# Two-map attention with three score banks in turn, one bank for transpositions, negated scaled keys and one reciprocal per step

## The reference

```
def diff_attention(q, k, v, qn_g, kn_g, lam_vec, subln_g, lambda_init):
    q = partial_rope(rmsnorm(q, qn_g)) * (A_DIM ** -0.5)      # [B, T, 4 heads, 2 maps, 64]
    k = partial_rope(rmsnorm(k, kn_g))
    v = ...                                                   # [B, 4 heads, T, 128]
    lam = exp(sum(lv[0] * lv[1])) - exp(sum(lv[2] * lv[3])) + lambda_init
    for each block of 128 queries:
        s = einsum('bhcqd,bhckd->bhcqk', q_block, k)          # c: the two maps
        p = softmax(where(causal, s, NEG_BIG), axis=-1)
        a = p[:, :, 0] - lam * p[:, :, 1]
        o = einsum('bhqk,bhkv->bhqv', a, v)
    return rmsnorm(o, subln_g) * (1.0 - lambda_init)
```

## Time and profile before

| what | us |
|---|---|
| median of 3 runs (lowest to highest) | 3673.33 (3672.34 to 3683.07) |
| the profiled execution | 3681.57 |
| its span on the core | 3679.8 |
| mean granted TensorE clock | 0.963 of 2.4 GHz |
| first reduction of the stage to the end of its last copy out, layer 0 | 67.16 |
| the same, layer 1 | 65.92 |

### The profile page before, as it was taken

The page is one execution under the profiler, slowest core; times in us unless marked ns, Lnnn a source line. Parts: engine busy times, 40 slices in busy tenths (PEclk is TensorE's granted clock), DMA queues, the critical chain, the costliest instruction groups (busy, mean ns, idle before and its releaser), DMA issues.

```text
span 3679.8 us, 41482 instructions
## 1 busy us (share of the span) xinstructions
PE 3533.7 (96%) x16488; PEld 2783.2 (76%) x16488; DVE 1470.8 (40%) x2606; ACT 1008.7 (27%) x1246; POOL 1500.2 (41%) x505
## 2 busy tenths in 40 slices
PE   8999999799999999999999999988999999789999
PEld 7878777578887888765788876845888869448887
DVE  4454267844243423235311146765201267643010
ACT  2222222622223212204222233342212333422121
POOL 3444452035454545510355554402546445015453
PEclk9999998999999999999999999978999999779999
DMA  6434221024352434211223222201222212002222
GB/s 245 179 140 190 97 81 68 1 82 194 120 195 97 183 131 153 86 56 50 80 84 105 85 92 79 71 1 46 92 93 101 91 69 81 12 35 90 93 95 76
DMA packets 53867, 360.66 MB, mean 98 GB/s; under 512 B 5968, under 2 KB 6352, under 8 KB 16592
## 3 DMA queue, kind: packets, MB, share of 16 engines
q1 hardware_dynamic: 53712, 358.53, 26.6%
HBM read 356.41 MB, written 2.10 MB: 97 GB/s over the span
## 4 chain that ended last, share of the span: by engine, by line
PE 90%; DVE 6%; ACT 1%; issue 1%; DMA 1%; POOL 1%; SPq 0%; DVEq 0%; ACTq 0%; POOLq 0%
PE LP L500 79%; PE XB L500 9%; DVE S L2116 1%; PE XB L711 1%; DMA big<-w_ada 1%; PE LP L827 1%; POOL w_lo L1618 1%; ACT E L1172 1%; DVE tmp L2238 0%; DVE st L2236 0%; DVE gain L1951 0%; ACT sq L1172 0%; DVE wk L2136 0%; DVE stat L2128 0%; DVE ada_in L2605 0%
## 5 line engine op out<-in xcount | busy, mean ns | idle before, releaser
L1618 POOL TENSOR_TENSOR w_lo<-ring,w_hi 128x2048 fp32r<-128x2048 f32 (+1 forms) x263 | 1125.8, 4281 | 724.5 <-ACT w_hi L1172 724.1
L500 PE MATMUL LP<-u_hi,w_hi 128*128 128x512 f32 x2480 | 987.3, 398 | 17.7 <-ACT u_hi L1172 10.6
L500 PE MATMUL LP<-u_hi,w_lo 128*128 128x512 f32 x2480 | 975.0, 393 | 0.0
L500 PE MATMUL LP<-u_lo,w_hi 128*128 128x512 f32 x2480 | 947.7, 392 | 0.0
L500 PE MATMUL LP<-big_r,w_hi 128*128 128x512 f32 x2432 | 750.0, 389 | 1.2 <-POOL w_lo L1618 1.2
L1172 ACT ACTIVATE w_hi<-ring 128x2048 fp32r<-128x2048 f32 (+1 forms) x263 | 468.6, 1782 | 827.8 <-PE LP L500 734.2
L500 PE MATMUL LP<-big_r,w_lo 128*128 128x512 f32 x1472 | 576.4, 392 | 0.0
L500 PEld LDWEIGHTS LP<-u_hi,w_hi 128*128 128x128 f32 x2480 | 471.8, 190 | 133.0 <-issue 35.8
L500 PEld LDWEIGHTS LP<-u_hi,w_lo 128*128 128x128 f32 x2480 | 471.5, 190 | 101.1
L500 PEld LDWEIGHTS LP<-u_lo,w_hi 128*128 128x128 f32 x2480 | 470.1, 190 | 96.1 <-issue 0.5
L500 PEld LDWEIGHTS LP<-big_r,w_hi 128*128 128x128 f32 x2432 | 455.9, 188 | 95.7 <-issue 1.2
(11 more groups left out here) (306 smaller groups left out, 3622.2 us busy)
## 6 DMA issues: line engine op xcount, KB each, us to landing
ada_in<-w_ada SPq DMA_DIRECT2D x66, 1024.0 KB, 4.9
ring<-w_in SPq DMA_DIRECT2D x22, 1024.0 KB, 4.7
ring<-w_gu00a SPq DMA_DIRECT2D x11, 1024.0 KB, 7.2
ring<-w_gu00b SPq DMA_DIRECT2D x11, 1024.0 KB, 6.7
ring<-w_gu01a SPq DMA_DIRECT2D x11, 1024.0 KB, 6.8
ring<-w_gu01b SPq DMA_DIRECT2D x11, 1024.0 KB, 6.7
ring<-w_gu10a SPq DMA_DIRECT2D x11, 1024.0 KB, 6.8
ring<-w_gu10b SPq DMA_DIRECT2D x11, 1024.0 KB, 7.0
```

Source lines behind the costliest of these rows:

```text
L500: return pe.matmul(o, lhsT=lhsT, rhs=rhs, start=start, stop=stop)
L1618: gp.tensor_tensor(w_lo[:, slab % RING, 0:width], ring[:, slab % RING, 0:width], w_high(q, width).bitcast(F32), ALU.subtract).then_inc(s(" ...
```

## The change

The two-map attention gets functions of its own (`diff_attention`) on TensorE, ScalarE and VectorE, with their own semaphores; `attention` keeps the one-map case. What differs for the two maps:

- The scores go through three PSUM banks in turn (`XB[k % 3]`), and TensorE waits for the reduction of three maps before; all transpositions go to `XB[3]`, so that each waits for ScalarE's copy of the one before.
- The keys are multiplied by their gains and by -0.125 (L2490 has a second factor), and the causal mask is negated once; the reduction takes the minimum of the negated scaled scores, and that minimum serves as the bias of the exponential, whose scale is -1. The small instruction L2119 is gone, and with it the `link` behind the reduction.
- The two sums are inverted by one instruction on two columns; minus lambda is a second factor of the instruction that scales map 1.

```diff
-                            if k >= 2:
-                                pe.wait_ge(s("smax_done"), k - 1)
-                            score(hh, m, qb, XB[k % 2]).then_inc(s("scores_done"), 1)
+                            k = 2 * n + m
+                            if k >= 3:
+                                pe.wait_ge(s("diff_max"), u0 + k - 2)
+                            score(hh, m, qb, XB[k % 3]).then_inc(s("diff_scores"), 1)
...
-                        if k >= 2:
-                            pe.wait_ge(s("pt_done"), k - 1)
-                        pe.wait_ge(s("probs_done"), k + 1)
-                        src = wk[:, 4 + k % 2, :] if maps == 2 else E[:, k % 4, :]
+                        if i:
+                            pe.wait_ge(s("pt_done"), p0 + i)
+                        pe.wait_ge(s("probs_done"), p0 + i + 1)
                         for b in range(qb + 1):
-                            last = pe.transpose(XB[2 + k % 2][:, blk(b)], src[:, blk(b)], cc("ident"))
+                            last = pe.transpose(XB[3][:, blk(b)], wk[:, 4 + i % 2, blk(b)], cc("ident"))
...
+                        if n >= 2:
+                            act.wait_ge(s("probs_done"), p0 + n - 1)
+                        for m in range(2):
+                            k = 2 * n + m
+                            act.wait_ge(s("diff_max"), u0 + k + 1)
+                            f(E[:, k % 4, 0:W], S[:, m, 0:W], ACT.Exp, scale=-1.0, bias=stat[:, k % 4, 0:1],
+                              accum_out=stat[:, k % 4, 1:2]).then_inc(s("diff_exp"), 1)
...
+                        f(ET[:, i % 2, 0:W], XB[3][:, 0:W], ACT.Copy).then_inc(s("pt_done"), 1)
...
+                link(ts(cc("causal"), cc("causal"), -1.0, None, ALU.mult))
...
-                            link(dve.tensor_tensor_reduce(
-                                out=S[:, k % 2, 0:W], in0=XB[k % 2][:, 0:W], in1=mask(qb, W), scale=1.0,
-                                scalar=LOWEST, op0=ALU.add, op1=ALU.max, accum_out=stat[:, k % 4, 2:3]))
-                            ts(stat[:, k % 4, 0:1], stat[:, k % 4, 2:3], -scale, None, ALU.mult)\
-                                .then_inc(s("smax_done"), 1)
+                            dve.tensor_tensor_reduce(
+                                out=S[:, m, 0:W], in0=XB[k % 3][:, 0:W], in1=cc("causal", T - W, W), scale=1.0,
+                                scalar=-LOWEST, op0=ALU.add, op1=ALU.min, accum_out=stat[:, k % 4, 0:1])\
+                                .then_inc(s("diff_max"), 1)
...
-                            link(dve.reciprocal(stat[:, q % 4, 3:4], stat[:, q % 4, 1:2]))
-                            link(ts(stat[:, q % 4, 3:4], stat[:, q % 4, 3:4], lam, None, ALU.mult))
-                            link(ts(wk[:, 3, 0:W], E[:, 2 * k % 4, 0:W], stat[:, q0 % 4, 3:4], None, ALU.mult))
+                        link(dve.reciprocal(stat[:, e:e + 2, 3:4], stat[:, e:e + 2, 1:2]))
+                        link(ts(wk[:, 3, 0:W], E[:, e + 1, 0:W], stat[:, e + 1, 3:4], lam, ALU.mult, ALU.mult))
...
-                        ts(big[:, c:c + 2, :], LP[p][:, :, :], sp_("qn" if k < 3 else "kn", l), None, ALU.mult)\
+                        gains, sign = (sp_("qn", l), 1.0) if k < 3 else (sp_("kn", l), -0.125)
+                        ts(big[:, c:c + 2, :], LP[p][:, :, :], gains, sign, ALU.mult, ALU.mult)\
```

More of the change, by code:

```diff
@@ L682, in rotate, with diff_attention, attention @@
                 pl.rope += len(chunks)
-            def attention(heads, score, val, hd, maps=1, beside=None):
+            def diff_attention(l, score, val, beside):
+                n_units = DIFF_H * NB
+                u0, p0, h0 = 2 * l * n_units, pl.prob, pl.head
+                for n in range(n_units + 3):
+                    if n < n_units:
+                        hh, qb = divmod(n, NB)
+                        for m in range(2):
[3 more added lines that the diff above has]
+                            score(hh, m, qb, XB[k % 3]).then_inc(s("diff_scores"), 1)
+                        beside(n)
+                    if 0 <= n - 2 < n_units:
+                        i, qb = n - 2, (n - 2) % NB
+                        if i:
+                            pe.wait_ge(s("pt_done"), p0 + i)
+                        pe.wait_ge(s("probs_done"), p0 + i + 1)
+                        for b in range(qb + 1):
+                            last = pe.transpose(XB[3][:, blk(b)], wk[:, 4 + i % 2, blk(b)], cc("ident"))
+                        last.then_inc(s("transposed"), 1)
+                    if n >= 3:
+                        i = n - 3
+                        hh, qb = divmod(i, NB)
+                        if qb == 0 and h0 + hh >= 2:
+                            pe.wait_ge(s("o_taken"), h0 + hh - 1)
+                        pe.wait_ge(s("pt_done"), p0 + i + 1)
+                        for b in range(qb + 1):
+                            last = mm(LP[0][:, (h0 + hh) % 2, blk(qb)], val(hh, b), ET[:, i % 2, blk(b)],
+                                      start=b == 0, stop=b == qb)
+                        last.then_inc(s("pv_done"), 1)
+                pl.prob += n_units
+                pl.head += DIFF_H
+            def attention(heads, score, val, hd):
                 per = P // hd
@@ L695, in attention @@
                         hh, qb = divmod(n, NB)
[L696 to L702 removed]
+                        k = u0 + n
+                        if k >= 2:
+                            pe.wait_ge(s("smax_done"), k - 1)
+                        score(hh, qb, XB[k % 2]).then_inc(s("scores_done"), 1)
                     if 0 <= n - 2 < n_units:
@@ L723, in attention @@
                         last.then_inc(s("pv_done"), 1)
-                pl.unit += n_units * maps
+                pl.unit += n_units
                 pl.prob += n_units
@@ L1340, in attention @@
                     if n < n_units:
[L1341 to L1353, removed]
+                        W, k = (n % NB + 1) * P, u0 + n
+                        act.wait_ge(s("smax_done"), k + 1)
+                        if p0 + n >= 4:
+                            act.wait_ge(s("transposed"), p0 + n - 3)
+                        f(E[:, (p0 + n) % 4, 0:W], S[:, k % 2, 0:W], ACT.Exp, scale=scale, bias=stat[:, k % 4, 0:1],
+                          accum_out=stat[:, k % 4, 1:2]).then_inc(s("exp_done"), 1)
                     if n >= 2:
@@ L1360, in attention @@
                         f(ET[:, k % 2, 0:W], XB[2 + k % 2][:, 0:W], ACT.Copy).then_inc(s("pt_done"), 1)
-                    if beside:
-                        beside(n)
-                pl.unit += n_units * maps
+                    beside(n)
+                pl.unit += n_units
                 pl.prob += n_units
@@ L1563, in _ @@
                 layer(f"inv{l}", last=True, behind=behind_values)
-                attention(DIFF_H, 0.125, P, maps=2)
+                diff_attention(l)
                 for n in range(2 * NB):
```

88 lines of the change are left out of this document (62 added, 26 removed).

## The result

The changed kernel takes 3660.26 us in the median of 5 runs (3651.22 to 3660.47), the kernel before 3676.06 on the same chip (3672.34 to 3683.07): a ratio of 0.9947 with a 95% interval of 0.9937 to 0.9958. That is 0.53% less by the ratio (19.5 us, with an interval of 15.4 to 23.2) and 15.8 us by the medians, where 14.0 us were forecast. The gain is real and larger than forecast. The median lies within 1 us of the forecast all the same, since the kernel before came out at 3676.06 us here and the forecast was subtracted from 3673.3.

The account below looks back on a forecast made before the run. Bound: VectorE and TensorE handing dependent pieces back and forth, neither full, in two stages of 133 of 3680 us. Layer gains of 6.8 and 7.2 us, together 14.0, from 3673.3 gave 3659.3, put at 3659.5; range 3650 to 3668.

Parts of the forecast that it names:

- The steps of VectorE: VectorE's step in the two-map attention stages: fewer small instructions save 0.81 us each, between 0.62 and 0.87.
- The rival that counts only the time of the removed instructions: VectorE's steps: each saves only 0.64 us, 11.2 us in all, giving 3662 us; chance 0.07.
- What is lost on the way: Steps off the chain that ended last save nothing: 8 steps pay in layer 0, 8.5 in layer 1.
- The clock goes up: TensorE in both stages: less waiting may keep its clock up, another 5.7 us, giving 3654; chance 0.16.
- a sign against itself: TensorE's clock in the two stage windows under 0.70 or over 0.85 would show the forecast wrong.
- a sign of being right: The two stage windows, 67.2 and 65.9 us before, would be 60 and 59 us long.
- The lower end of the range: Put at 3650 us; all 16 steps paying with half the clock rise, 26.5 us or 3647, was the extreme.
- The start of the stage: Unit 1's scores, both maps together and sooner through three banks: 0.6 us gained per layer, between 0 and 1.15.
- The single bank: One bank for transpositions, each waiting for ScalarE's previous copy: costs 0.3 us a layer, between 0 and 2.6.
- TensorE becomes the bound: Both stages: TensorE sets the pace or its clock stays down, gain 10.3 or 8.4 us, 3663 or 3665; chance 0.24.
- the slower rival: Transpositions in one bank uncovered in all 32 steps: costs 27.8 us against 14.0, giving 3687; chance 0.03.
- VectorE's waits for scores: A sign of the forecast being right: these waits in the stage become longer than 7.1 us.

Follow-up runs that it names:

- e9: The kernel before plus idle TensorE products at more places, 45 a layer: 3659.87 us, ratio 0.9953.
- e6: The changed kernel plus 28 idle TensorE products a layer ahead of its waits: 3648.11 us, ratio 0.9924 to the kernel before.
- e2: The kernel before with only the minima (negated keys and mask, minimum reduction, no L2119): 3666.77 us, ratio 0.9972.
- e3: The kernel before with only one reciprocal for both sums and lambda as second factor: 3667.20 us, ratio 0.9971.
- e7: The kernel before with the single reciprocal and lambda factor in only the 8 units a layer counted as on the chain: 3672.41 us, ratio 0.9993.
- e8: The kernel before with the single reciprocal and lambda factor in only the other 8 units a layer: 3676.96 us, ratio 1.0005.
- e5: The kernel before plus 28 idle TensorE products a layer ahead of its waits: 3673.31 us, ratio 0.9993.
- e4: The changed kernel with the banks of before, two for scores and two for transpositions: 3659.72 us, ratio 0.9948 to the kernel before.
- e11: The changed kernel with unit 0's exponentials ahead of the one on Z and idle TensorE products in and behind the stage: 3648.39 us, ratio 0.9921.

## Why the prediction was right

The time was right, and so were the price of a step and the place where most of the gain came from. The sum under it was not in all its terms: the start gave nothing, the single bank cost nothing, the steps gave more, and a rival came on top. That the median is within 1 us of the forecast is luck in part. The forecast gain of 14.0 us lies outside the interval of the measured one (15.4 to 23.2 us). By the medians the gain was 1.8 us larger than forecast, and the kernel before was 2.7 us slower than in the three runs that the forecast was subtracted from: the two nearly cancel.

**The steps of VectorE: right, to 0.01 us.** Both distances are those taken from `duo_attention`, the second factor costs the 0.06 us, and the account at full clock gives 13.2 us for 16 steps against 13.0. The rival that counts only the time of the removed instructions (0.64 us a step) has the busy time right, which falls by 9.7 us (10.6 without the slow scaling, 0.66 a step), but as the whole it is out: the gaps between linked instructions give 2.6 us more. This is shown by the pair e9 and e6, and for each edit alone by e2 and e3, which have 1.86 and 1.85 us from the first reduction with W = 512 to the scaling instruction, in place of 2.30.

**"What is lost on the way": too small a count.** The prediction took 8 and 8.5 steps, since TensorE's run between the scores of unit 9 and unit 10 "is not shortened". It was: that run lay at half clock, and in the kernel after it is at full clock. TensorE's place on the chain was a matter of its clock, not of its work. With the clock equal, all 16 steps count, and 3.8 us of new waits and 0.8 us of the slow scaling come back, so that a layer gains 8.6 us in place of 6.8 and 7.2. This is the term that was mis-sized: 17.2 us measured in the windows for 14.0. At the clock that the changed kernel really had, e7 and e8 do not settle the count.

**"The clock goes up": it came besides.** The rival was put at 5.7 us and a chance of 0.16. It is worth 5.2 us in the windows (14.3 us lost to the clock before, 9.2 after), and it came with the forecast and not in its place. The clock of the windows, 0.87 and 0.85, reached and passed the 0.85 that the prediction named as a sign against itself, and the stages of 54.6 and 56.2 us are not the 60 and 59 that it named as a sign of being right. That shorter waits raised it from 0.75 to 0.87 is argued, from e5 and e9, where filled waits raise it with VectorE unchanged. How much of it a median holds stays open, because the clock's pieces fall differently from execution to execution. Together, 14.0 + 5.7 would have been 3653.6 us by the prediction's own terms; the ratio's 19.5 us fit that better than the 14.0. The lower end of the range was said to hold half of this rival, but its sum, 26.5 us, has the 16 steps alone.

**"The start of the stage": wrong.** 0.6 us a layer was forecast and nothing came. TensorE did have the scores earlier. But VectorE's reduction then waits for ScalarE, which is busy with Z for 1.06 us, and the scaling instruction meets GpSimd and loses 0.84 us. The bound of nothing was in the prediction; neither cause was.

**The single bank: right in kind, nothing in price.** ScalarE's copy releases the transposition in the steps behind W = 512, as forecast. e4 shows that it costs nothing: with two banks the stages are the same to 0.06 us. That the product behind the transposition needs that copy anyway is the likely reason, and was not tested by itself.

**"TensorE becomes the bound" and the slower rival** did not come. VectorE's waits for scores, forecast to grow over 7.1 us in layer 0, are 6.0 us there; at equal clock they grow from 1.1 to 2.9.

## What to carry to other kernels

In a stage where engines hand small pieces round, ask of each wait for TensorE whether TensorE is slow for its work or for its clock: the chain of one execution shows the clock's places as if they were work, and counts too few steps for the others. Idle products of TensorE ahead of its longest waits settle it, if there are enough of them: in the kernel before 28 a layer were worth nothing that could be told and 45 were worth 0.47%, nearly the 0.53% of the rewriting. In the kernel after 28 were worth another 0.2 to 0.3%. Windows of one execution show such gains larger than the whole program does, so both belong side by side. And a start-to-start distance of the same sequence elsewhere in the program is a better price than a sum of instruction times.

## What was not expected of the hardware

- An instruction of VectorE with 128 columns takes 1.19 or 1.37 us in place of 0.34 when it comes up while GpSimd multiplies two tiles in SBUF; it ends 0.08 to 0.15 us behind GpSimd's. Reductions that read PSUM (0.42 us) and scalings of one column (0.15 us) beside the same multiplications in the kernel before kept their times.
- TensorE's clock fell to 0.50 while it was busy without a gap: in the midst of the products of 4 rows behind the stage (4x512, from 2437.85 in e6 and 2436.16 in e11, half clock from about 2439.6 and 2438.5), although the stage ahead of them had been at 1.00 for 50 us. In e6 an idle time of 0.78 us lies ahead of these products. By the Trainium skill, "TensorE: Matmul & The Clock Gate", Part 1, it is idleness that lowers the clock; what lowered it here no run settles.
